# One TensorE visit for all three dense logits tasks, with the dense-attention chain behind it two to three pieces later

## What is computed

```python
def block(args):
    qb, tpos = args
    allowed = schunk[None, :] <= (tpos // CHUNK)[:, None]
    logits = jnp.einsum('bqhcd,bshcd->bchqs', qb, k).astype(jnp.float32) * (HEAD_DIM ** -0.5)
    logits = jnp.where(allowed, logits, NEG_INF)
    probs = jax.nn.softmax(logits, axis=-1)
    attn = (probs[:, 0] - lam * probs[:, 1]).astype(v.dtype)
    return jnp.einsum('bhqs,bshe->bqhe', attn, v)
...
out = _rmsnorm(out, sub_g) * (1.0 - lam_init)
```

## Time and profile before

| | us |
|---|---|
| median of 3 runs | 360.63 |
| lowest, highest | 360.16, 361.81 |
| the profiled execution's own time | 360.35 |
| its span, first to last instruction | 358.5 |
| PE busy in the span | 349.6 (98%) |
| DVE busy | 264.2 (74%) |
| ACT busy | 228.6 (64%) |
| POOL busy | 67.4 (19%) |

### The profile page before, as it was taken

How to read it: one execution, slowest core, us unless ns; L and a number is a source line. 1 busy time by engine, 2 the same in 40 slices (tenths; PEclk the granted TensorE clock), 3 DMA queues, 4 the chain that set the end, 5 groups by cost and what they waited for, 6 DMA issues and landing times.

```text
span 358.5 us, 5709 instructions
## 1 busy us (share of the span) xinstructions
PE 349.6 (98%) x1927; PEld 291.8 (81%) x1927; DVE 264.2 (74%) x562; ACT 228.6 (64%) x459; POOL 67.4 (19%) x121
## 2 busy tenths in 40 slices
PE   8899999999999999999999999999999999999992
PEld 7797888888887888888888888788888888888882
DVE  2786979988955766786787577988895668668543
ACT  2897557686587954655667564787658686365221
POOL 1066352132200000003005524014230000000000
PEclk9999999999999999999999999999999999999997
DMA  7996479862754455557574937546355547550011
GB/s 256 380 359 191 122 227 176 282 176 64 195 169 137 148 181 170 192 169 155 187 222 146 341 101 202 163 124 178 111 158 155 160 129 224 175 167 12 0 47 72
DMA packets 31948, 61.12 MB, mean 170 GB/s; under 512 B 2376, under 2 KB 4688, under 8 KB 31920
## 3 DMA queue, kind: packets, MB, share of 16 engines
q1 hardware_dynamic: 30640, 56.96, 50.3%
q0 software_dynamic: 1120, 3.28, 4.6%
q10 hardware_dynamic: 160, 0.53, 0.5%
HBM read 59.71 MB, written 1.05 MB: 169 GB/s over the span
## 4 chain that ended last, share of the span: by engine, by line
PE 93%; DMA 2%; issue 2%; ACT 1%; DVE 0%; SPq 0%; DVEq 0%; POOLq 0%; POOL 0%
PE proj L1230 25%; PE proj L1232 25%; PE proj L1231 25%; PE sc L1311 3%; DMA raw<-in_w_ple_proj_dram 2%; PE tr L1372 2%; PE sc L1163 2%; PE tr L1329 2%; PE pv L1393 2%; PE pv L1388 1%; PE proj L1147 1%; PE proj L1174 1%; PE proj L1163 1%; PE proj L1136 1%; PE sc L1260 0%
## 5 line engine op out<-in xcount | busy, mean ns | idle before, releaser
L1230 PE MATMUL proj<-w_hi,act_hi 128*128 128x512 f32 (+1 forms) x392 | 157.4, 401 | 0.0
L1232 PE MATMUL proj<-w_hi,act_lo 128*128 128x512 f32 (+1 forms) x392 | 152.2, 388 | 0.0
L1231 PE MATMUL proj<-w_lo,act_hi 128*128 128x512 f32 (+1 forms) x392 | 151.7, 387 | 0.0
L832 DVE TENSOR_TENSOR w_lo<-raw,w_hi 128x1024 fp32r<-128x1024 f32 (+1 forms) x102 | 121.4, 1208 | 12.1 <-ACT w_hi L592 11.5
L592 ACT ACTIVATE w_hi<-raw 128x1024 fp32r<-128x1024 f32 (+2 forms) x103 | 102.6, 1023 | 6.8 <-DMA raw<-in_w_ple_proj_dram 4.1
L1232 PEld LDWEIGHTS proj<-w_hi,act_lo 128*128 128x128 f32 x392 | 73.6, 188 | 15.5
L1230 PEld LDWEIGHTS proj<-w_hi,act_hi 128*128 128x128 f32 x392 | 73.7, 188 | 14.6 <-issue 1.0
L1231 PEld LDWEIGHTS proj<-w_lo,act_hi 128*128 128x128 f32 x392 | 73.8, 188 | 12.8
L533 POOL TENSOR_TENSOR rstd<-var,minus_half 128x1 f32<-128x1 f32 x12 | 7.6, 639 | 192.6 <-DVE var L820 162.8
L729 ACT ACTIVATE probs<-probs,neg_max 128x128 f32<-128x128 f32 (+1 forms) x64 | 28.2, 444 | 6.0 <-DVE neg_max L983 6.0
L523 POOL TENSOR_TENSOR v_all<-work,rot_tab 128x128 f32<-128x128 f32 x16 | 10.6, 662 | 77.6 <-ACT work L592 77.4
(11 more groups left out here) (209 smaller groups left out, 440.5 us busy)
## 6 DMA issues: line engine op xcount, KB each, us to landing
raw<-in_w_in_dram SPq DMA_DIRECT2D x59, 512.0 KB, 4.2
raw<-in_w_out_dram SPq DMA_DIRECT2D x16, 512.0 KB, 3.3
raw<-in_w_ple_gate_dram SPq DMA_DIRECT2D x16, 512.0 KB, 3.8
raw<-in_w_in_dram SPq DMA_DIRECT2D x7, 324.0 KB, 5.0
raw<-in_w_ple_proj_dram SPq DMA_DIRECT2D x4, 512.0 KB, 3.5
probs<-in_w_in_dram SPq DMA_DIRECT2D x2, 512.0 KB, 9.3
g_ple<-in_ple_norm_g_dram POOLq DMA_DIRECT2D x2, 512.0 KB, 7.2
g_norm<-in_post_norm_g_dram POOLq DMA_DIRECT2D x2, 512.0 KB, 9.2
```

What stands on the lines that cost most here:

```text
L832: nc.vector.tensor_tensor(w_lo[:, g % SLOTS, 0:nk * cols], landing(g, nk * cols), w_hi[:, g % SLOTS, 0:nk * cols].bitcast(fp32), ALU.subtr ...
L1230: nc.tensor.matmul(ps, src_hi[:, b, k0 + k, :], hi, start=(first_u and k == 0), stop=False)
L1231: nc.tensor.matmul(ps, src_hi[:, b, k0 + k, :], lo, start=False, stop=False)
L1232: last = nc.tensor.matmul(ps, src_lo[:, b, k0 + k, :], hi, start=False, stop=last_k)
```

## The change

The matmuls of task 0 move from behind piece 12 to the visit behind piece 15, ahead of those of tasks 1 and 2, and are written to the banks `tr` and `pv` instead of `sc0` and `sc1`. The softmax, mixing, transposing and value steps that follow move two to three pieces later, lambda two earlier, the third exponentials one earlier. The transposes `T QA,0` move from 25 to 23 and `T QA,1` from 29 to 30; `hv` goes from 21 and 27 to 23 and 30, `hn` from 23 and 29 to 25 and 31. The rounds of `topk` stay.

```diff
 PLACE = dict(
-    lam=15,
+    lam=13,
     QB=[5, 3],
     KB=[9, 12],
-    QA=[25, 29],
+    QA=[23, 30],
     KA=[32, 37],
-    S=[12, 15, 18, 34, 42, 43],
-    E=[13, 16, 24, 36, 42, 43],
-    R=[16, 16, 19, 19, 24, 24, 40, 43, 44, 44, 44, 45],
-    PT=[19, 23, 26, 40, 41, 45, 46, 50, 51],
-    PV=[20, 25, 28, 42, 52, 52],
+    S=[15, 17, 20, 34, 42, 43],
+    E=[15, 18, 23, 36, 42, 43],
+    R=[18, 18, 21, 21, 24, 24, 40, 43, 44, 44, 44, 45],
+    PT=[21, 25, 28, 40, 41, 45, 46, 50, 51],
+    PV=[22, 27, 30, 42, 52, 52],
     glu=46,
-    hv=[21, 27],
-    hn=[23, 29],
+    hv=[23, 30],
+    hn=[25, 31],
...
-S_WITH = {1: 2, 4: 5}
+S_VISIT = {0: [0, 1, 2], 3: [3], 4: [4, 5]}
...
         def s_bank(i):
 
-            return proj[2 + i % 2] if i // 2 in S_WITH.values() else sc[i % 2]
+            if i // 2 == 0:
+                return [tr, pv][i]
+            return proj[2 + i % 2] if i // 2 in (2, 5) else sc[i % 2]
...
                     if s[1] == 0:
                         pe.wait_ge(relu_done, L * 4 + 4)
+                        pe.wait_ge(tr_out, tr_index(L, ("T", "KB", 1)))
+                        pe.wait_ge(z_out, L * 8 + 2)
+                    elif s[1] == 3:
+                        pe.wait_ge(qk_hi_done, L * 6 + QK_SPLIT.index(("KA", 0)) + 1)
+                        pe.wait_ge(max_done, L * 12 + 4)
                     else:
...
+                    for n in S_VISIT[s[1]]:
+                        g, b, _, keys = s_task(2 * n)
+                        logits(L, n, g, b, keys)
```

More of the change, by code:

```diff
@@ L1344, in _ @@
                                     ins.then_inc(dots_done, 1)
-                elif kind == "S" and s[1] not in S_WITH.values():
+                elif kind == "S" and s[1] in S_VISIT:
                     g, b, _, keys = s_task(2 * s[1])
[L1347 to L1351, removed]
                     if s[1] == 0:
                         pe.wait_ge(relu_done, L * 4 + 4)
-                    else:
[L1355 to L1362, removed]
+                        pe.wait_ge(tr_out, tr_index(L, ("T", "KB", 1)))
[3 more added lines that the diff above has]
+                        pe.wait_ge(max_done, L * 12 + 4)
+                    else:
+                        pe.wait_ge(tr_out, tr_index(L, ("T", "KA", 1)))
+                        pe.wait_ge(max_done, L * 12 + 8)
+                    for n in S_VISIT[s[1]]:
+                        g, b, _, keys = s_task(2 * n)
+                        logits(L, n, g, b, keys)
                 elif kind == "PT":
```

## The result

| | before | changed |
|---|---|---|
| median (lowest to highest) of 6 runs, us | 360.39 (359.9 to 361.81) | 367.16 (365.78 to 372.0) |
| the profiled execution's own time, us | 360.35 | 372.0 |
| its span, us | 358.5 | 370.2 |
| PE busy | 349.6 (98%) | 354.0 (96%) |
| mean granted clock | 0.994 | 0.982 |

The changed kernel takes 1.0194 times as long, with a 95% interval of 1.0155 to 1.0233, that is 7.0 us more; the ratio leaves out the slowest execution of the six (372.0 us), and the medians of all six differ by 6.8 us. The profiled execution is that slowest one, so it shows more than the median has.

What follows compares the result with a forecast made beforehand. PE's own issue was taken to bound the kernel: 360.35 us plus 5.4 for waits at `PV 1` less 0.7 for the merged visit gives 365.05, predicted as 365.2 us. The range of 8 in 10 was 363.4 to 369.0 us.

Steps and rivals of the forecast that it cites:

- The bound: PE, busy 98% of the span, is the sum of its own issue; nothing behind a wait gives it back.
- The wait at `PV 1`: `PV 1` waits for the first head norm, now behind mixing and two selection rounds on DVE: 2.7 us a layer.
- the nine terms of the chain: Steps in series on ACT and DVE from `PV 0`'s start to the head norm's end: 11.32 us, against PE's 8.66.
- The merged visit: Task 0 shares the visit of tasks 1 and 2, saving one change to 64 rows and back: 0.34 us a layer.
- the 0.41 us: Full gain a layer of the shared visit if only changes of row mode cost and the type turn is free.
- The clock: Rival: the granted clock falls in the wait at `PV 1`, 1.7 us more a layer, 368.6 us; chance 0.33.
- Lambda two pieces earlier fits in DVE's time before task 0's logits arrive: Step on DVE: moving lambda two pieces earlier was claimed to fit before task 0's logits; no cost was given.
- about one microsecond: Margin left at `PT 0`, which needs the first mixing, with six pieces instead of seven less the visit; costs nothing while held.
- More waits: Rival: `T KA,0` or `PT 0` also runs late, a few tenths up to 1 us a layer, 366 to 367 us; chance 0.09.
- the forecast by itself: Wait of 2.3 to 3.1 us in each layer with the clock kept: 364.2 to 366.1 us; chance 0.48.

Runs made afterwards that it cites:

- e4: Changed kernel with the first head norm one step earlier and layer 0's small loads for lambda issued earlier; 359.48 us, on another chip 358.7 us.
- e2: Changed kernel with only the first head norm put back one step earlier (hv 22, hn 24), lambda staying at step 13; 361.52 us, ratio 1.006.
- d0: Changed kernel with lambda's small loads issued earlier and no selection round between task 2's mixing and the late head norm; 361.48 us, ratio 1.0032.
- d3: Changed kernel with lambda's small loads issued earlier and three selection rounds ahead of the late head norm; 369.74 us, ratio 1.0276.
- e7: The changed kernel unaltered, run once more beside the kernel before; 369.16 us, ratio 1.0218.
- e5: Against e4, the merged visit undone: task 0 alone behind piece 14, tasks 1 and 2 behind piece 15; 360.38 us, ratio 1.0011.
- d2: Changed kernel with only lambda's small loads issued earlier, two selection rounds ahead of the late head norm as in the change; 366.5 us, ratio 1.0171.
- e6: The kernel before with only lambda moved two steps earlier, from 15 to 13; 361.91 us, ratio 1.0042.

## Why the prediction was right, and where it was not

**The bound.** That PE is the sum, so that a wait there comes back in full, held: e4 without waits is at the kernel before less the merged visit, and the account of the changed kernel closes to 0.2 us.

**The wait at `PV 1`.** Shown. Forecast 2.7 us a layer, measured 2.69 and 2.60; it goes away with the head norm one step earlier (e2, e4) and follows the rounds ahead of it (d0 to d3). The sum of the nine terms of the chain was right to 0.05 us in e7's layer 0.

**The merged visit.** Forecast 0.34 us a layer, measured 0.38, in the changed kernel and in e5. From task 0's last pair (60.41) to the second matmuls of tasks 1 and 2 (60.65) are 0.24 us, and elsewhere in the visit such two steps take 0.11 and 0.12: the turn from plain fp32 to fp32r on 64 rows costs next to nothing. What is paid are the turns between 128 and 64 rows. The Trainium skill (TensorEngine Tiling (Array Packing), Key Properties) says that changing the tiling mode, and not just the tile, drains TensorE; of a change of type it says nothing there. The trace agrees: the 0.41 us that I had worked out by that rule was nearer than my 0.34, and the row decides for 0.38.

**The clock.** A rival with a chance of 0.33, and it does occur, but not as I put it. I took it as a matter of one forecast or the other, 1.7 us in each layer or none. In the runs it is a matter of the execution, and the wait at `PT 0`, which I did not have, can bring it down too. The price of one fall behind a wait of this length, 1.7 us, was about right (1.6). The Trainium skill (TensorE: Matmul & The Clock Gate, Part 1) tells of the idle array's fall to half rate; the rows show 0.50 behind some of the waits and none behind others.

**The step that failed** is "Lambda two pieces earlier fits in DVE's time before task 0's logits arrive", and with it the margin of "about one microsecond" at `PT 0`. I counted DVE's time, which is indeed free from 58.25, and not the load that lambda reads. Before, DVE asked for it at 63.37 and it had landed at 61.6, so nothing in the list of waits told of it. In the changed kernel DVE is there 3.8 us early. What slack there was behind it takes up 1.5 us of that, and 2.3 us arrive at PE. Layer 1, whose load has long landed, has no such wait. The Trainium skill (DMA: Bandwidth & Descriptors, Anatomy of one DMA — SWDGE (gpsimd) path) fits one transfer issued by GpSimd as 2.0 us and the bytes by 436 KB/us; for the 64 KB of `g_sub` that makes an estimate of 2.2 us, by which lambda would not have waited. The trace doesn't agree, it has 8.5 us for the last of several small loads in a row, and it decides. This is what "More waits" named in general, at 1 us a layer; its place was right and its cause was not seen. It puts the forecast at 365.2 + 2.3 = 367.5, and the medians are 367.16 and 369.16: the second is about one fall above that. e4 against e2 shows it as 2.0 us, d2 against the changed kernel as 0.7 or 2.7, depending on which of its two medians is taken.

**How much of it was luck.** The way and the main cause were not. But 365.2, and the 364.2 to 366.1 us of the forecast by itself, lie below both medians. The range up to 369.0 was made wide for the clock, and in the first six runs it is, by the account, the wait at `PT 0` that fills it; the second median, 369.16, lies just outside.

**Open.** What decides in which execution a wait of 2.5 us brings the clock down; d0's median, 1.1 us over the kernel before where two waits (1.4) less the gain (0.8) make 0.6, which is what its profiled execution has (360.99 us); and e6's remainder.

## What to carry to other kernels

Before a step is moved earlier, look up when the load that it reads is issued and when it lands: a load that lands 2 us before its reader is in no list of waits, and is the first thing to bite. Where an in-order engine releases a bank, count all that stands ahead of the release in its queue, in series from the last event that both orders share; here that was right to 0.05 us and pointed at a one-step mend, which took +7 us down to +1.5 and, with the load asked for earlier, to between -0.5 and -1.0. When TensorE is the bound, price a new wait of over 2 us with its possible clock fall as well, and expect a spread between executions.

## What the runs showed of the hardware

- The last of five small loads issued on POOL in a row took long to land: `g_sub`, 128x128, 8.5 us from issue to landing in layer 0 of the changed kernel and 6.5 in layer 1 (6.1 to 9.1 in all profiles; the four of `lam_in` before it 3.9 to 6.9 in the changed kernel), and 0.54 us of POOL to issue.
- PE's waits of up to 1.6 us never brought the clock down in these profiles. Of the twelve listed with 2.0 to 2.7 us seven did and five did not, with the same program (three falls in the first profile of the changed kernel, none in the second). Both of 3.6 us did, for 6.8 us instead of 3.4.
- The change of rows of the array costs 0.38 us for going to 64 and coming back; the change from plain fp32 to fp32r on the same rows about 0.01 (0.24 us where 0.11 and 0.12 are usual).
